# Expert rows added to gathered residual rows and scattered out unit by unit, in place of a final pass by token tile

## What is computed

```python
x = x + gate1 * mix
h = rmsnorm(x, norm2_g) * (1.0 + scale2) + shift2
x = x + gate2 * hier_moe(h, ...)
y = rmsnorm(x, final_g)

def hier_moe(h, ...):
    gsel = argmax(xt @ router_gw + router_gb)            # one of 4 groups
    topv, topi = top_k(softmax(le_of_that_group), 2)     # two of its 4 experts
    hid = einsum('nd,edf->nef', xt, exp_w13)             # 16 experts, D_EXPERT 256
    a, bgl = split(hid, 2)
    act = silu(a) * bgl * gate[:, :, None]
    return einsum('nef,efd->nd', act, exp_w2)
```

## Time and profile before

| | |
|---|---|
| runs | median 636.88 us of 3 (636.16 to 638.16) |
| profiled execution, its own time | 636.54 us |
| its span, first to last instruction | 634.7 us |
| PE busy | 563.8 us, 89% of the span |
| DVE, ACT, POOL busy | 244.5, 179.3, 51.8 us |
| mean granted TensorE clock | 0.963 of full speed |
| HBM | 112.36 MB read, 18.65 MB written |

### The profile page before, as it was taken

One profiled execution on the slowest core, in us unless ns is written; L12 is line 12 of the kernel. 1 busy time (PEld: TensorE's weight loads), 2 busy tenths in 40 slices (PEclk: granted clock), 3 DMA queues, 4 the chain that ended last, 5 costly groups with the idle time before them and its releaser, 6 DMA issues.

```text
span 634.7 us, 6208 instructions
## 1 busy us (share of the span) xinstructions
PE 563.8 (89%) x2374; PEld 301.4 (47%) x2374; DVE 244.5 (39%) x518; ACT 179.3 (28%) x327; POOL 51.8 (8%) x68
## 2 busy tenths in 40 slices
PE   0799999999998999999999996879999999999414
PEld 0345545554445665566455554634544545444201
DVE  0430747956206642111455557251121211211077
ACT  5321289963312202244211112101111011110122
POOL 3000000002402200000000000110010100100140
PEclk9999999999999999999999998599999999999857
DMA  7969166119729523200076000599999999952293
GB/s 290 387 198 326 52 201 230 34 36 350 264 79 329 187 69 108 76 1 0 1 279 252 33 34 34 177 401 399 370 375 375 360 374 368 373 216 84 74 357 132
DMA packets 79471, 131.42 MB, mean 207 GB/s; under 512 B 8185, under 2 KB 35154, under 8 KB 79442
## 3 DMA queue, kind: packets, MB, share of 16 engines
q1 hardware_dynamic: 73256, 108.96, 49.5%
q0 software_dynamic: 3744, 13.63, 5.6%
q10 hardware_dynamic: 2442, 8.43, 3.3%
HBM read 112.36 MB, written 18.65 MB: 206 GB/s over the span
## 4 chain that ended last, share of the span: by engine, by line
PE 56%; DVE 6%; ACT 2%; issue 1%; DMA 1%; POOL 1%; POOLq 0%; DVEq 0%; ACTq 0%
PE ms L1338 17%; PE ps L1272 11%; PE ps L1359 9%; PE ps L1008 8%; PE ps L1321 2%; PE ps L1208 1%; PE ms L1243 1%; PE ps L1413 1%; DMA wring<-expert_rows,yidx 1%; PE ps L1198 1%; POOL wring L685 1%; PE ps L1157 1%; DVE tmp L1658 1%; PE ms L1311 1%; DVE tmp L1628 1%
## 5 line engine op out<-in xcount | busy, mean ns | idle before, releaser
L1008 PE MATMUL ps<-r,wring 128*128 128x512 f32 (+1 forms) x512 | 143.4, 437 | 2.7 <-DVE r L1477 1.1
L1008 PEld LDWEIGHTS ps<-r,wring 128*128 128x128 f32 x512 | 78.8, 191 | 67.8 <-issue 65.3
L1272 PE MATMUL ps<-wring,mixT 128*128 128x512 f32 x160 | 72.1, 599 | 0.5 <-DVE tmp L1749 0.5
L1338 PE MATMUL ms<-wring,tmp 128*128 128x512 f32 x128 | 57.7, 593 | 1.3 <-DVE tmp L1908 1.3
L1272 PEld LDWEIGHTS ps<-wring,mixT 128*128 128x128 f32 x160 | 29.2, 190 | 32.0 <-issue 31.3
L1922 DVE COPY gd<-ps 128x256 f32<-128x256 f32 x16 | 6.8, 424 | 89.9 <-PE ps L1348 89.9
L658 POOL DMA_INDIRECT mixT<-h_rows,slot_tok x16 | 15.2, 951 | 317.1 <-DVE slot_tok L1848 181.0
L956 ACT ACTIVATE tmp<-ms 128x256 f32<-128x256 f32 x16 | 6.1, 384 | 120.5 <-PE ms L1338 120.5
L1338 PEld LDWEIGHTS ms<-wring,tmp 128*128 128x128 f32 x128 | 23.6, 190 | 27.9 <-issue 26.3
L1082 PE MATMUL ps<-wring,r 128*128 128x512 f32 x80 | 35.6, 598 | 0.4 <-issue 0.4
L1028 PE MATMUL ps<-wring,cs 128*32 128x512 f32 x192 | 23.4, 626 | 12.5 <-DMA wring<-in_ada_w_dram 11.0
(11 more groups left out here) (293 smaller groups left out, 714.7 us busy)
## 6 DMA issues: line engine op xcount, KB each, us to landing
wring<-in_ada_w_dram SPq DMA_DIRECT2D x12, 2048.0 KB, 13.1
wring<-in_exp_w_dram SPq DMA_DIRECT2D x8, 2048.0 KB, 15.0
wring<-in_w_in_dram SPq DMA_DIRECT2D x16, 512.0 KB, 4.3
r<-in_exp_w_dram SPq DMA_DIRECT2D x4, 2048.0 KB, 14.4
wring<-in_exp_w_dram SPq DMA_DIRECT2D x8, 1024.0 KB, 8.3
tmp<-in_exp_w_dram SPq DMA_DIRECT2D x4, 2048.0 KB, 14.9
expert_rows<-tmp ACTq DMA_DIRECT2D x16, 512.0 KB, 7.4
expert_rows<-zero SPq DMA_DIRECT2D x9, 512.0 KB
```

Source lines behind the costliest of these rows:

```text
L1008: i = mm(d, lhsT, r, start=first, stop=last)
L1272: i = mm(product(f"mx{t}")[:, half * 512:(half + 1) * 512], mixT[:, k, t * P:(t + 1) * P], w[:, k, :], start=(k == 0), stop=(k == KD - 1))
L1338: i = mm(ms[:, b, :], xgT[:, b, k, :], e13[u % 4][:, k, :], start=(k == 0), stop=(k == KD - 1))
```

## The change

The ten gathers, the sums and the final norm by token tile are gone. In their place:

- The residual rows are stored to a DRAM tensor `residual_rows` (`xacc_d`) by SP, one DMA after each store of `h2` rows.
- For each unit POOL also gathers the residual rows of its tokens (`gather_residual`), into one of three buffers `xr` in the place of `xres`. DVE adds the expert's rows, times `gate2`, to them (`row_gates`, `add_rows`), out of PSUM; ACT no longer copies or stores them.
- POOL scatters the sum back to `residual_rows` (`put_back`) for the tokens of which this unit is the first expert. For the tokens of which it is the last, ACT squares (`row_roots`), DVE norms (`norm_rows`), and POOL scatters to the outputs (`give_out`, one DMA for each of the two outputs). The lists have numbers out of bounds at places that a DMA is to leave out, and the DMAs carry a bounds check, the gathers as well, so that unused places are not fetched.
- The experts are worked in another order, `order_of`: the first of each group, then the second of each, so that units of one group are four apart. The norm runs from unit 4 on.
- Which of a token's two experts comes last is found in `put` (five small DVE instructions for each tile in place of one in `choose`), and coded into the token number (+1024). `decode` takes it apart, with six small instructions after `activate(0)`.
- `count_units` is cut into three parts that follow `add_rows` of units 0, 1 and 2, without the two instructions for the row numbers. The clearing of overflow rows (nine SP DMAs of 512 KB between 86 and 203 us) is gone.

The core of the diff:

```diff
-            pool.wait_ge(zrow_out, 16 * (1 + NOV))
+            gather(0)
+            gather(1)
+            pool.wait_ge(x1_out, 16 * NT)
+            gather_residual(0)
+            gather_residual(1)
+            gather(2)
+            pool.wait_ge(decoded, 1)
             for u in range(NE):
-                gather(u)
+
+                if u > NG:
+                    give_out(u - 1)
+                put_back(u)
+                if u + 2 < NE:
+                    gather_residual(u + 2)
+                if u + 3 < NE:
+                    gather(u + 3)
+            give_out(NE - 1)
...
+            def gather_residual(u):
+
+                e = order_of[u]
+                if u >= 3:
+                    pool.wait_ge(back_out[u % 3], 16 * (u // 3))
+                if u >= 3 + NG:
+                    pool.wait_ge(normed, u - 3 - NG + 1)
+                pool.indirect_dma_start(xr[:, u % 3, :], None, xacc_d[:, :], rows_at(slot_tok[:, e:e + 1]),
+                                        bounds_check=N - 1, oob_is_err=False).then_inc(xr_in[u % 3], 16)
+
+            def put_back(u):
+                e = order_of[u]
+                pool.wait_ge(z_half, 2 * u + 2)
+                pool.indirect_dma_start(xacc_d[:, :], rows_at(back_row[:, e:e + 1]), xr[:, u % 3, :], None,
+                                        bounds_check=N - 1, oob_is_err=False).then_inc(back_out[u % 3], 16)
...
-                b = u % 2
-                if u >= 2:
-                    act.wait_ge(y_out[b], 16 * (u // 2))
-                for h in range(2):
-                    act.wait_ge(y_done, 2 * u + h + 1)
-                    A(ysb[:, b, h * 512:(h + 1) * 512], ps[:, 2, h * 512:(h + 1) * 512], ACT.Copy).then_inc(y_taken, 1)
-                act.wait_ge(y_taken, 2 * u + 2)
-                act.dma_start(y_d[u * P:(u + 1) * P, :], ysb[:, b, :]).then_inc(y_out[b], 16)
+                if u >= NG:
+                    row_roots(u)
...
+            def add_rows(u):
+
+                for h in range(2):
+                    cols = slice(512 * h, 512 * h + 512)
+                    dve.wait_ge(y_done, 2 * u + h + 1)
+                    tt_(g2[:, cols], ps[:, 2, cols], g2[:, cols], ALU.mult).then_inc(y_taken, 1)
+                    dve.wait_ge(y_taken, 2 * u + h + 1)
+                    if h == 0:
+                        dve.wait_ge(xr_in[u % 3], 16 * (u // 3 + 1))
+                    tt_(xr[:, u % 3, cols], xr[:, u % 3, cols], g2[:, cols], ALU.add).then_inc(z_half, 1)
...
+            def norm_rows(u):
+                dve.wait_ge(z_root, u - NG + 1)
+                link(V.reciprocal(un[:, 4, u:u + 1], un[:, 3, u:u + 1]))
...
+                stt(ob[:, u % 2, :], xr[:, u % 3, :], un[:, 4, u:u + 1], fing, ALU.mult, ALU.mult).then_inc(normed, 1)
...
             for u in range(NE):
                 take_a(u)
+                row_gates(u)
                 if u + 2 < NE:
                     take_x(u + 2)
+                if u > NG:
+                    norm_rows(u - 1)
                 if u + 1 < NE:
                     activate(u + 1)
+                add_rows(u)
+                count_units(u)
+            norm_rows(NE - 1)
```

More of the change, by code:

```diff
@@ L361, in hybrid_step @@
         h2_out = [sem(f"h2_out{i}") for i in range(2)]
-        zrow_out = sem("zrow_out")
+        x1_out = sem("x1_out")
+        decoded = sem("decoded")
+        xr_in = [sem(f"xr_in{i}") for i in range(3)]
+        back_out = [sem(f"back_out{i}") for i in range(3)]
+        z_half = sem("z_half")
+        z_sum = sem("z_sum")
+        z_root = sem("z_root")
+        normed = sem("normed")
+        rows_done = [sem(f"rows_done{i}") for i in range(2)]
         lfin_ready = sem("lfin_ready")
@@ L981, in _ @@
                         A(sact[:, 0, :], ms[:, 0, 0:DE], ACT.Silu).then_inc(ov["silu"], 1)
[L982 to L984 removed]
+                        act.wait_ge(ov["z"], i + 1)
+                        A(sq[:, :], xr[:, 0, :], ACT.Square, accum_out=un[:, 0, 0:1]).then_inc(ov["sq"], 1)
+                        act.wait_ge(ov["sq"], i + 1)
+                        A(un[:, 3, 0:1], un[:, 0, 0:1], ACT.Sqrt, bias=eps[:, 0:1], scale=1 / D).then_inc(ov["root"], 1)
+                        act.wait_ge(ov["out"], (i + 1) * 48)
                         act.sem_inc(ov_turns, 1)
                     act.nop()
[L987 to L991 removed]
         @block.tensor
@@ L1403, in _ @@
                         m.then_inc(ov["y"], 1)
-                        pe.wait_ge(ov["out"], (i + 1) * 16)
+                        pe.wait_ge(ov["out"], (i + 1) * 48)
                         pe.sem_inc(ov_turns, 1)
                     pe.nop()
-            for n, t in enumerate(PE_SUMS):
-                pe.wait_ge(yg_in[t], 32)
-                for half in range(2):
-                    cols = slice(half * 512, (half + 1) * 512)
-                    for j in range(2):
-                        m = mm(ps[:, n, cols], ident[:, :], yg[:, 2 * t + j, cols], start=(j == 0), stop=(j == 1))
-                m.then_inc(pair_sum, 1)
         @block.vector
@@ L1816, in put @@
                     mine.rearrange("p (i a) -> p i a", a=1).to_broadcast([P, 2, P]), ALU.is_equal).then_inc(placed, 1)
+                left, when, last, mark = (rt3[:, n, :].rearrange("p (i t) -> p t i", i=2)[:, t, :] for n in range(4))
+                link(ts_(when, mine, float(P), float(2 * EG), ALU.is_ge, ALU.mult))
+                link(tt_(when, when, left, ALU.subtract))
+                link(tt_(last, when, when[:, ::-1], ALU.is_gt))
+                link(ts_(mark, last, float(FIN), tokid[:, t:t + 1], ALU.mult, ALU.add))
+                tt_(tok_sel[:, :, t, :], r16[:, 0:2, t, :], mark.rearrange("p (i a) -> p i a", a=1).to_broadcast([P, 2, NE]),
+                    ALU.mult).then_inc(placed, 1)
             def gather_table(t):
@@ new lines, in _ @@
+                        dve.wait_ge(ov["y"], i + 1)
+                        tt_(g2, ps[:, 2, :], g2, ALU.mult).then_inc(ov["yg"], 1)
+                        dve.wait_ge(ov["yg"], i + 1)
+                        dve.wait_ge(ov["gx"], (i + 1) * 32)
+                        tt_(xr[:, 0, :], xr[:, 0, :], g2, ALU.add).then_inc(ov["z"], 1)
+                        dve.wait_ge(ov["root"], i + 1)
+                        V.reciprocal(un[:, 4, 0:1], un[:, 3, 0:1]).then_inc(ov["rec"], 1)
+                        dve.wait_ge(ov["rec"], i + 1)
```

268 lines of the change are left out of this document (146 added, 122 removed).

## The result

The changed kernel takes 773.15 us (median of 4 runs, 771.53 to 776.96), against 637.06 us for the kernel before (4 runs, 636.16 to 638.16): 1.211 times as long, with an interval of 1.205 to 1.217. The forecast was 722 us in a range of 682 to 762. The sign and the kind of loss are as forecast, the size is not.

What follows compares the result with a forecast made beforehand. PE bounds the expert stage, busy 20.00 of 20.00 us; a 39.2 us tail follows. 636.5 - 28.8 (tail) - 0.7 (routing and unit 0) + 114 (13 ring passes) = 721, given as 722 us, range 682 to 762.

Steps and rivals of the forecast that it cites:

- The ring: Expert stage: output, add, put back, gather, transpose, output; 18.3 us, 20.2 at lowered clock, against 11.4; 13 passes, +114 us.
- Term 4: Expert stage: the gather of h2 rows lands 6.3 us after its start, bounds 4.1 and 8.5.
- Terms 2 and 3: Expert stage: POOL wakes in 0.27 us, issues two DMAs in 2.48; gather begins 4.2 after T, the output's end.
- Term 5: Expert stage: PE's clock halves after idling 6.9 us, costing 0.9 + 1.0 = 1.9 us a pass, bounds 0.9 and 3.2.
- The additions to each unit as throughput: Expert stage: about 5.5 us more on DVE and 6.2 on POOL fit into a unit's 11.39 us, costing nothing.
- The tail: After the last output product: 10.4 us (8.6 to 12.1) instead of 39.2, a gain of 28.8 us.
- Routing and unit 0: Ahead of the expert stage: +1.4 us from DVE instructions, PE's 2.11 us wait gone; net -0.7 us, bounds -2 and +1.4.
- both high bounds: Expert stage: with landing and clock loss both at their upper bounds, a pass loses 12.3 us, 160 us in all.
- Quick landing: Rival, expert stage: gathers find empty queues and land in 4.1 us; a pass loses 6.6, total 693 us; chance 0.14.
- Dear scatters: Rival: bounds-checked or DRAM-destination DMAs take POOL twice as long to issue, +2.5 us a pass, 754 us; chance 0.10.
- A clock that stays low: Rival: PE's clock does not recover between idle stretches, 7.74 us more a pass instead of 1.9, 798 us; chance 0.05.
- Not slower: Rival: the gather comes within 3.65 us of the output's end, no stall, kernel at 607 us; chance 0.03.

Runs made afterwards that it cites:

- Experiments 2 to 4: Changed kernel with gather(u+3) first after the z_half wait, 723.76 us; with weight loads held until the gather landed, 735.74 us; with both edits, 673.70 us.
- Experiment 5: Changed kernel with 11 unused matmuls (6 in the last two units) on PE after turn_a: 748.61 us.
- experiment 1: Changed kernel with gather(u+3) moved to the front of POOL's iteration, ahead of give_out and put_back: 617.12 us, 0.966 times the kernel before.
- the fourth experiment: Changed kernel with gather(u+3) as POOL's first DMA after z_half and SP's weight loads held until the gather landed: 673.70 us.
- the second experiment: Changed kernel with gather(u+3) still waiting for z_half, but issued ahead of put_back and gather_residual: 723.76 us.

## Why the prediction was right and wrong

**The ring**: right. It was found from the order of POOL's instructions, and it is there, 13 times, with the instructions that the prediction named.

**Term 4, the landing of 6.3 us**: this is the step that failed. The 11 passes that start weights at T land in 8.6 to 10.3 us, median 9.5, and the last two, which start none, in 5.2 and 5.3:

```profile
704.26 5.19 DMA mixT<-h_rows,slot_tok
...
724.63 5.28 DMA mixT<-h_rows,slot_tok
```

Against 6.3 that is 11 x 3.2 - 2 x 1.1 = 33 us. The prediction argued that in a longer unit "they have time to drain" and went below its own loaded rows of 7.5 and 8.5. The time between bursts was there (the DMA share of the stage is 0.45, below the 0.6 forecast), but it is no help to a transfer issued 4.85 us behind the start of the burst. The ring ties the gather to T, and SP's wait for `output` ties the weights to T: the two collide in each of the 11 passes that load weights. The prediction saw both facts and did not add them up. It also read 8.5 as an upper bound, which the trace of before could not give: none of its gathers stood third behind two other transfers of POOL's. Experiments 2 to 4 price these two parts.

**Terms 2 and 3, POOL's wake and issues**: a little small. From the end of DVE's add (582.13) POOL took 0.78 us to the first DMA (582.91) instead of 0.27, and spaced the DMAs by 1.28 and 1.34 instead of 1.24. The gather began at T + 4.85 (580.68 to 585.53), forecast T + 4.2: 0.65 x 13 = 8 us. The 0.27 was from a DMA with one wait; the chain shows that before L678 an instruction of its own takes the wait and 0.5 us pass behind it.

**Term 5, the cold clock**: nearly right. Transposes at half clock cost 1.97 - 0.87 = 1.1 us more. The half product took 3.9 to 5.5 us in place of 3.44, on average 4.48, so 1.0 more. That is 2.1 a pass; forecast was 0.9 + 1.0 = 1.9, and 13 x 0.2 = 3 us are the difference. Experiment 5 gave back 1.9, since its transposes still took 1.09.

**The additions to each unit as throughput**: right, shown by experiment 1 with units of 11.39 us.

**The tail**: its working held, with an item missing. DVE's last scaling ended at T + 5.1 (forecast 4.4), the scatters stood at T + 5.9 and T + 7.2 (forecast 4.7 and 5.9). POOL had been idle for 1.27 us before the first and took 0.8 us from DVE's end at 761.41 to it, where the forecast had 0.3:

```profile
762.21 0.98 POOL L684 DMA_INDIRECT out_dram<-xres,tmp  x1 [1.27 <-DVE xres L2017]
763.49 0.97 POOL L686 DMA_INDIRECT out_dram<-xres,tmp  x1 [0.30 <-issue]
```

They landed sooner, in 3.0 us instead of 4.5 (763.49 to the DRAIN at 766.5), and POOL's DRAIN began at T + 10.2, against 10.4. Then came its 5.95 us, which the prediction did not have. The profile of before had a DRAIN, but hidden: it ended before SP did. So the tail gained 22.9 us, not 28.8.

**Routing and unit 0**: forecast -0.7, measured +0.5. The 2.11 us wait of PE is gone as expected. But the gate table ended 1.6 us later, and the first hidden product took longer at a low clock, 8.99 us against the 7.83 of the earlier trace rows.

Together, on the spans: 46 us in the ring (160.3 against 114; 33, 8 and 3 of them are accounted for above, 2 are not), 5.9 in the tail, 1.2 ahead of them, 53 in all; the forecast of the sum was 84.5 more than before, and 137.9 was measured. Seen as a whole, the stage's +160 us stands exactly where the prediction's own sum of both high bounds stood ("12.3, 160 us"). That is a coincidence, since the landing was above its bound of 8.5 and the cold clock below its 3.2. The range did not reach there, because it was cut after two rivals that each moved a single cost.

**The rivals.** Quick landing: fell; even in the last two passes the landing was 5.2 us, not 4.1. Dear scatters: fell; the trace gives a scatter to `residual_rows` in 0.98 us (median, 0.97 to 1.59), so POOL's cost is that of a gather. A clock that stays low: fell in every pass, though the clock took until about halfway through the product on average to come back. Not slower: fell with the changed order as it is, and holds at once when the gather goes first. The prediction put that kernel at 607, and experiment 1 has 617, with the 5.9 us of the DRAIN as the largest known part of the difference. In its trace `output(0)` also ends 3.0 us later than in the kernel before (435.40 against 432.41), and from the end of `output(14)` to that of `output(15)` it takes 5.57 us, where the kernel before took 4.45.

What stays open is part of why the traffic of a pass takes so long, where the prediction took 3 MB of weights at 377 GB/s for 8 us. From 580.7 to 595.1 us all transfers together moved 4.02 MB, which at 377 GB/s would be 10.7 us and took 14.4, 278 GB/s on average; the three transfers that POOL issued then landed only 8.2, 8.9 and 9.6 us after their issue. Why the rate fell to 229 and 164 GB/s at 585 and 586 us, with the engines' share at 0.80 and 0.89, and how the packets of the two queues are dealt out among the 16 engines, no run shows. Nor was the DRAIN measured with more than 72 DMAs.

## What to carry to other kernels

A prefetch in an in-order queue has the lead that the waits ahead of it leave it. Before adding a wait on a result to a queue that also prefetches, count what stands behind it; issue the prefetch first, since the same work with one line moved was 3.4% faster than before in place of 21% slower. When a transfer comes onto the critical path, price it by the moment at which it is issued and by what is issued with it, not by the mean load of the stage. And let an engine that has issued many DMAs by software not be the one that finishes last.

## What the runs showed of the hardware that was not expected

- Where all its transfers have landed, POOL ends with a DRAIN of 83 to 84 ns for each indirect DMA of 144 packets that it issued in the whole program (27, 54 and 72 DMAs: 2.27, 4.48 and 5.95 us), whether the last one was a gather or a scatter. It added to the time only where POOL ended last.
- An indirect gather of some 80 rows of 4 KB lands in 4.3 us (median of the fourth experiment) with the weights held back, and in 9.5 some 5 us behind the start of a burst of 3 MB and behind two other transfers of POOL's; in the first experiment, with the DMA engines at a share of 0.96 (500 to 520 us), it is 8.7.
- Rows whose number is out of bounds are not moved: POOL's queue moved 15.75 MB in 72 DMAs, which is 3840 rows of 4 KB (twice 1280 gathered, twice 640 scattered), but each DMA still has 144 packets (10368 / 72).
- A DMA issued by POOL with a bounds check costs it 0.97 to 1.04 us in these passes, and 1.33 where a DVE instruction over 1024 columns runs beside it (L662 at 585.53, beside L1997 at 584.70). In the second experiment, with another order, L662 took 1.03 and it was `gather_residual` that stood beside that instruction: 1.32 us at 599.45, beside L1998 at 598.59.
